# Sixteen experts of a routed layer: the prompt tokens of four experts gathered and transposed together, and the splits dealt out anew

## What is computed

```
cap = max(1, EC_CAPACITY * n_tok // N_EXPERTS)
gate, idx = lax.top_k(aff.T, cap)
xe = jnp.take(t, idx, axis=0)
hid = jax.nn.silu(jnp.einsum("ecd,edf->ecf", xe, w_gate)) * jnp.einsum("ecd,edf->ecf", xe, w_up)
ye = jnp.einsum("ecf,efd->ecd", hid, w_down) * gate[..., None]
out = jnp.zeros_like(t).at[idx.reshape(-1)].add(ye.reshape(-1, D))
```

## Time and profile before

| what | value |
|---|---|
| median of three runs | 2628.82 us (2626.8 to 2632.13) |
| profiled execution | 2628.52 us |
| its span, first to last instruction | 2626.9 us |
| granted TensorE clock, mean of the span | 0.955 |
| TensorE, VectorE, ScalarE, GpSimd busy | 92%, 48%, 35%, 17% |
| DMA over the span | 342.67 MB, mean 130 GB/s |

### The profile page before, as it was taken

The page is one execution under the profiler, slowest core; times in us unless marked ns, Lnnn a source line. Parts: engine busy times, 40 slices in busy tenths (PEclk is TensorE's granted clock), DMA queues, the critical chain, the costliest instruction groups (busy, mean ns, idle before and its releaser), DMA issues. The chain is left out here.

```text
span 2626.9 us, 37764 instructions
## 1 busy us (share of the span) xinstructions
PE 2413.2 (92%) x14495; PEld 2089.7 (80%) x14495; DVE 1258.8 (48%) x1813; ACT 913.1 (35%) x1452; POOL 441.4 (17%) x306
## 2 busy tenths in 40 slices
PE   5999998999899999999999799149999999999997
PEld 4876675666688888888778688149999999999997
DVE  6334345445423230000154433866766767667764
ACT  6333334334500011211210222125555555555552
POOL 0001111110300000000000000023344444344342
PEclk6999998998999999999999899569999999999999
DMA  5300000001011112222155444348888888888882
GB/s 168 102 27 25 17 25 16 17 25 41 1 44 37 40 32 86 78 90 90 66 173 165 174 138 136 112 141 257 263 252 258 255 269 260 248 249 270 262 257 53
DMA packets 328236, 342.67 MB, mean 130 GB/s; under 512 B 11856, under 2 KB 308816, under 8 KB 327632
## 3 DMA queue, kind: packets, MB, share of 16 engines
q1 hardware_dynamic: 315280, 309.96, 37.4%
q0 software_dynamic: 12864, 31.46, 4.7%
HBM read 297.35 MB, written 44.04 MB: 130 GB/s over the span
## 5 line engine op out<-in xcount | busy, mean ns | idle before, releaser
L1969 PE MATMUL bank_pair<-tokens_hi_lo,ehi 128*128 128x320 f32 x2048 | 533.7, 347 | 1.1 <-DVE tokens_hi_lo L1838 1.1
L1970 PE MATMUL bank_pair<-tokens_hi_lo,elo 128*128 128x160 f32 x2048 | 483.7, 236 | 0.0
L1970 PEld LDWEIGHTS bank_pair<-tokens_hi_lo,elo 128*128 128x128 f32 x2048 | 392.3, 192 | 0.0
L1969 PEld LDWEIGHTS bank_pair<-tokens_hi_lo,ehi 128*128 128x128 f32 x2048 | 385.5, 188 | 1.2 <-issue 1.2
L1776 ACT ACTIVATE ehi<-eraw 128x2048 fp32r<-128x2048 f32 x192 | 362.8, 1905 | 39.3 <-PE bank_pair L1970 29.4
L1831 DVE TENSOR_TENSOR elo<-eraw,ehi 128x2048 fp32r<-128x2048 f32 x144 | 328.5, 2282 | 19.7 <-ACT ehi L1776 19.7
L1752 POOL TENSOR_TENSOR elo<-eraw,ehi 128x2048 fp32r<-128x2048 f32 x47 | 225.5, 4798 | 314.0 <-ACT ehi L1776 314.0
L1969 PE MATMUL bank_pair<-hidden_hi_lo,ehi 128*128 128x320 f32 x1024 | 269.3, 348 | 0.0
L1970 PE MATMUL bank_pair<-hidden_hi_lo,elo 128*128 128x160 f32 x1024 | 241.4, 236 | 0.0
L1206 PE MATMUL bank_pair<-hT_hi,whi 128*128 128x512 f32 (+1 forms) x576 | 204.0, 354 | 1.2 <-PEq L1036 1.2
L1207 PE MATMUL bank_pair<-hT_lo,whi 128*128 128x512 f32 (+1 forms) x576 | 204.0, 354 | 0.0
(11 more groups left out here) (244 smaller groups left out, 4240.5 us busy)
## 6 DMA issues: line engine op xcount, KB each, us to landing
eraw<-in_w_eg SPq DMA_DIRECT2D x64, 1024.0 KB, 6.6
eraw<-in_w_eu SPq DMA_DIRECT2D x64, 1024.0 KB, 5.4
eraw<-in_w_ed SPq DMA_DIRECT2D x64, 1024.0 KB, 5.2
raw<-in_w_in SPq DMA_DIRECT2D x64, 512.0 KB, 4.2
scratch_g<-sig SPq DMA_DIRECT2D x24, 640.0 KB, 3.4
sig<-scratch_g SPq DMA_DIRECT2D x24, 640.0 KB, 3.9
xt<-in_x SPq DMA_DIRECT2D x10, 512.0 KB, 4.5
scratch_m<-acc SPq DMA_DIRECT2D x8, 640.0 KB, 5.0
```

Source lines behind the costliest of these rows:

```text
L1969: nc.tensor.matmul(out, wh, moving[:, k, :], start=(k == 0), stop=False)
L1970: ins = nc.tensor.matmul(out[:, HI], wl, moving[:, k, HI], start=False, stop=(k == KD - 1))
```

## The change

The rows of prompts are no longer gathered for each expert. Once for four experts (`PACK`), GpSimd gathers 4 times 32 rows into one tile of 128 partitions, with an index column in which the four experts' tokens stand below each other (`idx_rep`, built by four more small copies before the sample picks, and four copies instead of one behind the transposes). TensorE transposes them in eight full blocks into the PSUM pair that also takes `y_back` (`prompt_rows`, behind chunk 9 of every fourth expert), ScalarE copies the result into SBUF (`prompt_copy`), and each expert's part is split from there. The rows of samples are transposed by themselves, all eight blocks ahead of chunk 8, and split in two halves of 512 columns and one prompt part of 256 (ScalarE at chunks 9 and 10, VectorE at 9 and 11).

GpSimd's splits are those of the chunks 1, 5 and 9 instead of 3, 7 and 11. Its scatter stands behind its split of chunk 5 (at chunk 1), and its gather right behind the scatter (at chunk 2). VectorE copies the gather's indices at chunk 2. The loop over experts is written in groups of four: the first and the last four experts outside, two rounds of four inside.

```diff
@@ tiles @@
-    xg = [place("x_rows_s", [P, D]), place("x_rows_p", [CAP_P, D])]
+    xg = [place("x_rows_s", [P, D]), place("x_rows_p", [P, D])]
+    GROUPS = NEXP // PACK
+    xpT = at("x_prompt_T", [P, KD, P], F32, HT)
...
+    idx_rep = place("idx_repeated", [NEXP, PACK, CAP_P])
+    idx_c = [place("idx_cols_s", [CAP_S, NEXP], U32), place("idx_cols_p", [P, GROUPS], U32)]
-    XB = ((0, 3), (3, 6), (6, 8))
+    XB = ((0, 4), (4, 8))
+    HALF = 2
+    def by_pool(j):
+        return j % 4 == 1
...
     def run_experts(eng, body):
-        body(0, False, True)
-        body(1, True, True)
-        with eng.Fori(2, NEXP - 1) as e:
-            body(e, True, True)
-        body(NEXP - 1, True, False)
+        for i in range(PACK):
+            body(i, i, 0, i > 0, True)
+        with eng.Fori(1, GROUPS - 1) as g:
+            for i in range(PACK):
+                body(PACK * g + i, i, g, True, True)
+        for i in range(PACK):
+            body(NEXP - PACK + i, i, GROUPS - 1, True, i < PACK - 1)
@@ GpSimd @@
-            def gather(e):
+            def gather(e, group):
                 pool.wait_ge(ig_ready, e + 1)
-                wait_apart(pool, x_tr, 3 * e, pool_passed)
-                for s in range(2):
-                    nc.gpsimd.indirect_dma_start(xg[s][:], ...
+                wait_apart(pool, x_tr, HALF * e, pool_passed)
+                nc.gpsimd.indirect_dma_start(xg[0][:], ...
+                if group is not None:
+                    wait_apart(pool, xp_tr, group, pool_passed)
+                    nc.gpsimd.indirect_dma_start(xg[1][:], ...
-                    if jn % 4 == 3 and (after or jn < NCH):
+                    if by_pool(jn) and (after or jn < NCH):
...
-                    if j == 0 and before:
+                    if j == 1 and before:
                         scatter(e - 1)
-                    if j == 3 and after:
-                        gather(e + 1)
+                    if j == 2 and after:
+                        gather(e + 1, g + 1 if i == PACK - 1 else None)
-            pool.wait_ge(e_hi, 4)
-            nc.gpsimd.tensor_tensor(elo[3][:], eraw[3][:], ehi[3][:].bitcast(F32), ALU.subtract).then_inc(e_lo_p, 1)
+            pool.wait_ge(e_hi, 2)
+            nc.gpsimd.tensor_tensor(elo[1][:], eraw[1][:], ehi[1][:].bitcast(F32), ALU.subtract).then_inc(e_lo_p, 1)
@@ ScalarE @@
+            def prompt_copy(group):
+                act.wait_ge(xp_tr, group + 1)
+                wait(act, x_lo, 3 * PACK * group)
+                nc.scalar.activation(xpT[:].rearrange("p k t -> p (k t)"),
+                                     pair_bank[:].rearrange("p a b -> p (a b)"), ACT.Copy).then_inc(xp_cp, 1)
+            def x_split(e, b, i, group):
+                if b < HALF:
+                    act.wait_ge(x_tr, HALF * e + b + 1)
...
+                    nc.scalar.activation(xp[:, k0:k1, 0:CAP_S], src, ACT.Copy).then_inc(x_hi, 1)
+                else:
+                    act.wait_ge(xp_cp, group + 1)
+                    nc.scalar.activation(xp[:, :, CAP_S:CAP], xpT[:, :, CAP_P * i:CAP_P * (i + 1)],
+                                         ACT.Copy).then_inc(x_hi, 1)
...
+                    if after and j == 9:
+                        x_split(e + 1, 0, nxt, g + (nxt == 0))
+                        x_split(e + 1, 1, nxt, g + (nxt == 0))
                     if after and j == 10:
-                        x_split(e + 1, 0)
-                        x_split(e + 1, 1)
-                    if after and j == 11:
-                        x_split(e + 1, 2)
+                        if nxt == 0:
+                            prompt_copy(g + 1)
+                        x_split(e + 1, 2, nxt, g + (nxt == 0))
...
+            prompt_copy(0)
             for b in range(3):
-                x_split(0, b)
+                x_split(0, b, 0, 0)
@@ VectorE @@
+                    nc.vector.tensor_tensor(xp[:, :, CAP + CAP_S:2 * CAP], xpT[:, :, CAP_P * i:CAP_P * (i + 1)],
+                                            xp[:, :, CAP_S:CAP].bitcast(F32), ALU.subtract).then_inc(x_lo, 1)
...
+                    if after and j == 11:
+                        x_split(e + 1, 2, nxt)
-                    if jn % 4 != 3 and (after or jn < NCH):
+                    if not by_pool(jn) and (after or jn < NCH):
                         lo(e, jn)
...
-                    if j == 3 and after:
-                        gather_index(e + 1)
-                    if after and j == 10:
-                        x_split(e + 1, 0)
-                        x_split(e + 1, 1)
-                    if after and j == 11:
-                        x_split(e + 1, 2)
+                    if j == 2 and after:
+                        gather_index(e + 1, g + 1 if nxt == 0 else None)
+                    if after and j == 9:
+                        x_split(e + 1, 0, nxt)
+                        x_split(e + 1, 1, nxt)
...
             for k in range(PACK):
+                nc.vector.tensor_copy(idx_rep[:, k, :], idx_r[1][:])
...
+            for k in range(PACK):
+                rows = slice(CAP_P * k, CAP_P * (k + 1))
+                nc.vector.tensor_copy(idx_c[1][rows, :], bank[5][rows, k:NEXP:PACK])
@@ TensorE @@
-            def x_rows(e, b):
...
+            def x_rows(e):
+                pe.wait_ge(gathered[0], 16 * e + 16)
...
+                for b, (k0, k1) in enumerate(XB):
+                    for k in range(k0, k1):
+                        ins = nc.tensor.transpose(bank[4 + b][:, (k - k0) * CAP_S:(k - k0 + 1) * CAP_S],
+                                                  xg[0][:, k * P:(k + 1) * P], ident[:])
+                    ins.then_inc(x_tr, 1)
+            def prompt_rows(group):
+                pe.wait_ge(gathered[1], 16 * group + 16)
+                wait(pe, y_rdy, 2 * (PACK * group - 1))
+                for k in range(KD):
+                    ins = nc.tensor.transpose(pair_bank[:, k // 4, (k % 4) * P:(k % 4 + 1) * P],
+                                              xg[1][:, k * P:(k + 1) * P], ident[:])
+                ins.then_inc(xp_tr, 1)
...
+                    if copied is not None:
+                        pe.wait_ge(xp_cp, copied)
...
                     if j == 8:
+                        if after:
+                            x_rows(e + 1)
                         pe.wait_ge(h_lo, 4 * e + 3)
...
-                    if after and j == 9:
-                        x_rows(e + 1, 0)
-                        x_rows(e + 1, 1)
-                    if after and j == 10:
-                        x_rows(e + 1, 2)
+                    if after and i == PACK - 1 and j == 9:
+                        prompt_rows(g + 1)
...
-            for b in range(3):
-                x_rows(0, b)
+            x_rows(0)
+            prompt_rows(0)
```

More of the change, by code:

```diff
@@ L1660, in kernel_body @@
     SCATTERED = (16, 16 * (KD // PACK))
[L1661 removed]
+    ig_cur = [place("idx_gather_s", [CAP_S, 1], U32), place("idx_gather_p", [P, 1], U32)]
     e_hi = sem("expert_hi")
@@ L1704, in _, with body @@
         def _(sp):
-            def body(e, _before, after):
+            def body(e, _i, _g, _before, after):
                 for j in range(NCH if after else NCH - NER):
@@ L1745, in scatter, with body @@
                                                          compute_op=ALU.add).then_inc(scattered[1], 16)
-            def body(e, before, after):
+            def body(e, i, g, before, after):
                 for j in range(NCH):
                     jn = j + AHEAD
-                    if jn % 4 == 3 and (after or jn < NCH):
+                    if by_pool(jn) and (after or jn < NCH):
                         pool.wait_ge(e_hi, NCH * e + jn + 1)
@@ L1764, in _ @@
                 pool.wait_ge(t_saved[h], 16 * (N4 // 2))
-            gather(0)
+            gather(0, 0)
             run_experts(pool, body)
@@ L1794, in y_out, with body @@
                 nc.scalar.activation(y_rows[s][:], src, ACT.Copy, scale=g_cur[s][:, 0:1]).then_inc(y_rdy, 1)
-            def body(e, before, after):
+            def body(e, i, g, before, after):
+                nxt = (i + 1) % PACK
                 for j in range(NCH):
@@ L1848, in column, with gather_index @@
                 return bass.ds(e, 1)
-            def gather_index(e):
-                for s in range(2):
-                    wait(dve, gathered[s], 16 * e)
-                    ins = nc.vector.tensor_copy(ig_cur[s][:], idx_c[s][:, column(e)])
+            def gather_index(e, group):
+                wait(dve, gathered[0], 16 * e)
+                ins = nc.vector.tensor_copy(ig_cur[0][:], idx_c[0][:, column(e)])
+                if group is not None:
+                    wait(dve, gathered[1], 16 * group)
+                    ins = nc.vector.tensor_copy(ig_cur[1][:], idx_c[1][:, column(group)])
                 ins.then_inc(ig_ready, 1)
@@ L1929, in _, with y_back @@
         def _(pe):
[L1930 to L1947 removed]
+            def x_rows(e):
+                pe.wait_ge(gathered[0], 16 * e + 16)
```

(10 more changed lines are left out.)

64 lines of the change are left out of this document (26 added, 38 removed).

## The result

The changed kernel takes 2591.99 us (median of 4 runs, 2588.97 to 2593.27), the kernel before 2627.94 (4 runs, 2626.80 to 2632.13): a ratio of 0.985, 95% interval [0.983, 0.987]. Its profiled execution took 2593.27 us with a span of 2591.7; before it was 2628.52 and 2626.9, so the two profiles that are compared here lie 35.2 apart.

The account below looks back on a forecast made before the run. TensorE, busy 92% of the span and fully in the expert stage, was taken to bound the kernel. Savings of 39.0 - 2.6 - 1.0 - 1.1 = 34.3 us gave 2594.5 us on the median's footing, range 2589 to 2607.

Parts of the forecast that it names:

- The start: From first gather's landing to first product of the expert stage: net -2.5 to +4.5 us, taken as 1.0 us later.
- The jump: End of the four-expert loop body, run twice: one jump back over four times the code, 1.1 us, bounds 0 and 4.
- The largest term, the transposes: TensorE, per expert: 3.35 us in two blocks removed, eight uniform transposes of 0.80 added; 2.6 saved, 15 times, 39.0 us.
- prompt blocks taken off: TensorE, every fourth expert: a prompt block of eight with its break costs 0.85 us, three times inside the stage, 2.6 us.
- order of GpSimd, scatters, gathers: GpSimd's moved splits, scatters and gathers lie beside TensorE; gather lands by T+29, chunk 8 wants it at T+33.7; cost nothing.
- The other branch: TensorE's block of eight transposes: at about 275 ns each it costs an estimated 2.2 us and most of the gain goes.
- a jump of over 4 us: Loop's end: a jump back this long would show the forecast wrong.
- the upper end of the range: Whole kernel: 3.5 and 2.9 us more, and 0.14 instead of 0.10 per transpose (5.8), give 2606.5 us.
- a DMA share of 0.88: DMA engines in the expert stage: share rises from 0.84 with 3% less time per expert, below full, costed at nothing.
- 1: Rival, TensorE's blocks: a large transpose costs 0.26 us by itself; 11 us less gain, 2618 us; chance 0.06.
- 2: Rival, expert's start: VectorE's index copies stand behind GpSimd's split of chunk 5; TensorE waits 1.6 us, 15 times; 2619; chance 0.06.
- 3: Rival, expert's start: GpSimd gets the port before VectorE's split of chunk 4; TensorE waits 2.7 us, 15 times; 2635; chance 0.04.

## Why the prediction came out as it did

Two terms of the sum failed. The start was costed at 1.0 us later, because the larger gather of prompts was to land 2.6 later; the first product came 1.8 earlier. The jump was costed at 1.1 us and cost 4.67. The largest term, the transposes, was right in mechanism and size.

| term of the sum, us saved | predicted | traces |
|---|---|---|
| transposes, prompt blocks taken off | 39.0 - 2.6 = 36.4 | 36.75 |
| start | -1.0 | +1.8 |
| jump back | -1.1 | -4.67 |
| order of GpSimd, scatters, gathers | 0 | 0 |
| end | not in the sum | +1.3 |
| sum | 34.3 | 35.2 |

*Transposes: right in mechanism and size.* A period lost 2.66 (predicted 2.6), a prompt block costs 0.84 (0.85). 15 x 2.66 - 3 x 0.84 is 37.4; the first expert gave less, 2.0 (first product to first block of results, 59.54 to 57.56). It starts at the half clock, which lasted some 6.6 us behind the first product in this execution and 5.2 before; in the second profile of the changed kernel it lasted 3.7, and the first expert took 56.17. Rows 5 were the right price for a block of eight of one size. The other branch, a block of 2.2 us by the 275 ns of the Trainium skill (TensorE: Matmul & The Clock Gate, Part 4: PE-mode transpose), is excluded here: a block with its break costs 0.84.

*The jump: the mechanism was foreseen, the term mis-sized*, and its upper bound of 4 too; a jump of over 4 us was among the signs of being wrong. I took 1.1 from a loop of another stage, where TensorE waited for its sequencer. Here it waits 2.7, and then pays a second price that the sum did not have at all: 1.9 at the lower clock in one execution, a second wait of 1.3 in the other.

*The start: wrong in sign, and the term that put the forecast too high.* I had the landing 2.6 later: it is 0.7 earlier (1742.03, against 1742.70 in the earlier trace rows), 0.2 if it is counted from the transposes of the indices. The 2.6 was a choice between 0 and 6 that no row gave. The gather of prompts did take longer to land (8.1 after its issue, 6.8 before), but it was issued 2.0 earlier, as GpSimd spent 2.05 instead of 4.26 on the gather in front of it. One more weight load in front of it, which the prediction feared, is not there: between the index copies and this gather SyncE issues two in either trace (1732.49 and 1734.70 before, 1732.74 and 1733.23 now). Nor did I see that the samples would be turned under that wait. The work from landing to first product is 5.2, where I had 3.9 to 4.7. The added copies behind the transposes of the indices cost 0.7, inside the 0.5 to 1.0 said for all seven: the copy of the gather's indices stands 1.9 behind the transposes of the indices instead of 1.2 (1728.35 to 1730.24, 1728.82 to 1730.01). The bounds of this term were added up wrongly, too: its parts give -2.0 to +5.3, not -2.5 to +4.5.

*The end: missing in the sum.* 1.3 us. From the last block of results to the end it is 16.0 to 16.7 in every trace of a kernel with the joint prompt rows and 17.5 to 17.6 in every one without, with either order of GpSimd (16.2 with the old order, 17.6 with the new order alone). So it belongs to the joint rows; by what path stays open.

That the sum comes so near is luck: the errors nearly cancel, +2.8 and +1.3 against -3.6. By the profiles it is 0.9 short. The ratio of 0.985, put on the median that the prediction started from, would be 2589.4, at the low end of the range; in the changed kernel run again the first product lies 2.8 us earlier still (1744.45), and so do the transposes of the indices ahead of it (3.0), in stages that the change doesn't touch; with that profile's span of 2587.2 the gain would be 39.7. So differences of a few us between executions aren't the change's. Two slips moved nothing: the upper end of the range adds up to 2606.7, not 2606.5, and a DMA share of 0.88 goes with 5% less time per expert, not 3% (measured: 0.86).

*The order: costed at nothing, and right, but the reason is narrower than I gave.* With the old transposes it costs nothing (ratio 1.0007). With the new ones it saves 20 us against the old order, since the new token splits move VectorE's work into GpSimd's. Taken by itself, the order looks idle, and the transposes without it are worth less than half as much.

*Rivals.* 1 fell by the block of 0.79 and by the transposes set apart. 2 had the right chain and a false condition (0.15, not a stall). 3 did not occur: in the steady stage TensorE's only wait of note is the jump's 2.7; VectorE's split of chunk 4 (2058.18) is ahead of GpSimd's (2059.37).

## What to carry to other kernels

Group TensorE's transposes by size, and price a block from a block of one size in the same trace. Before VectorE's order is changed, or a second SBUF input is given to one of its operations, list what GpSimd does at that moment, and test the parts of a change together as well as one by one: here the order of GpSimd was worth 0 alone and 20 us with the rest. A longer loop body is not free: count the jump back, with the clock that TensorE may lose behind it, and write the loop out where there are only two or three rounds.

## What the runs showed of the hardware that was not expected

- A jump back over the code of four experts stalls TensorE 1.5 to 2.7 us, and with what follows costs 3.4 to 4.7; 5.9 in the run where GpSimd's split is held back, which has waits of 2.61 and 2.23 there (58.42 against some 52.5). Over the code of one expert it costs nothing that shows.
- Behind 2.7 us without work TensorE went on at the lower clock for 3.7 us (0.54), from a stage that had been at 1.00 throughout. In the second profile of the same kernel it stayed at 1.00 behind 2.65, and in the loop of four experts with the old transposes it fell behind 1.5 and 1.7. In the run with idle products it fell to 0.53 behind two waits of 2.35 and 1.83 with eight transposes between them.
- A VectorE copy of 128x2 stood 4.55 us beside a GpSimd split; a copy of 128x1 at the same place took 0.15.
- The same twelve transposes cost 2.55 us alternating in size and 1.49 in four groups of three: 1.06 for eight changes of size fewer.
